# A chunked recurrence beside a convolution: the order of VectorE's work inside a round

## The reference, cut to what matters

```
# convolution branch
z = za * sigmoid(zb)
z = conv over time(z, conv_w[31 taps]) + conv_b        # each channel by itself

# recurrence, for each head, S is 64 x 64
for t in range(512):
    Sa = S @ a_t                                        # a = -kk
    S  = S * w_t + outer(Sa, b_t) + outer(v_t, k_t)     # b = kk * a
    y_t = S @ r_t
y = group_norm(y) * gn_g + gn_b
out = ((y + (sum(r * k * r_k)) * v) * g) @ w_o
```

## Time and profile before

| | us |
|---|---|
| median of 3 runs | 3665.07 (3653.8 to 3669.39) |
| the profiled execution, its own time | 3657.74 |
| its span in the trace | 3655.9 |
| the stage of the recurrence with its warm-up, from the trace's times | some 680 (2340 to 3020) |
| busy over the whole span: PE / DVE / ACT / POOL | 3305.3 / 2015.0 / 1299.8 / 374.7 |

### The profile page before, as it was taken

One profiled execution on the slowest core, in us unless ns is written; L12 is line 12 of the kernel. 1 busy time (PEld: TensorE's weight loads), 2 busy tenths in 40 slices (PEclk: granted clock), 3 DMA queues, 4 the chain that ended last, 5 costly groups with the idle time before them and its releaser, 6 DMA issues.

```text
span 3655.9 us, 51894 instructions
## 1 busy us (share of the span) xinstructions
PE 3305.3 (90%) x21498; PEld 2605.7 (71%) x21498; DVE 2015.0 (55%) x3571; ACT 1299.8 (36%) x2143; POOL 374.7 (10%) x334
## 2 busy tenths in 40 slices
PE   6898899999899999998986889879999889989998
PEld 4667777777585677777765666567777777768886
DVE  5455356653432466654555437678778762554443
ACT  3234232222223342223333135456555533323221
POOL 0001000000000000000001000055445420000000
PEclk9899899999898999999997989989999989999999
DMA  3220023442551124432310220221111102233231
GB/s 126 61 69 2 24 93 128 132 133 68 85 99 42 37 96 138 138 115 69 127 46 26 62 87 12 75 61 39 45 41 40 45 5 87 81 110 104 93 99 62
DMA packets 318856, 274.78 MB, mean 75 GB/s; under 512 B 10912, under 2 KB 310048, under 8 KB 317856
## 3 DMA queue, kind: packets, MB, share of 16 engines
q1 hardware_dynamic: 314368, 256.07, 23.2%
q10 hardware_dynamic: 4256, 15.40, 1.1%
HBM read 265.16 MB, written 6.29 MB: 74 GB/s over the span
## 4 chain that ended last, share of the span: by engine, by line
PE 76%; DVE 13%; ACT 6%; issue 3%; POOL 1%; DMA 1%; DVEq 0%; ACTq 0%; SPq 0%; POOLq 0%
PE ps L95 74%; DVE f L107 4%; DVE f L101 3%; DVE r L101 3%; ACT f L88 2%; PE ps L98 2%; ACT f L92 1%; ACT r L92 1%; DVE f L104 1%; ACT f L89 1%; ACT L88 1%; POOL f L101 1%; DVE f L113 1%; DVE f L110 1%; DMA f<-in_w_in_odd 0%
## 5 line engine op out<-in xcount | busy, mean ns | idle before, releaser
L95 PE MATMUL ps<-r,r 128*128 128x512 f32 x10368 | 2459.2, 396 | 124.8 <-DVE r L101 87.3
L95 PEld LDWEIGHTS ps<-r,r 128*128 128x128 f32 x10368 | 1925.1, 190 | 601.7 <-issue 182.9
L95 PE MATMUL ps<-f,f 64*64 64x64 f32 (+9 forms) x10192 | 809.2, 270 | 181.2 <-ACT f L92 45.9
L101 DVE TENSOR_TENSOR r<-f,r 128x1024 fp32r<-128x1024 f32 (+2 forms) x621 | 657.4, 1064 | 461.7 <-ACT r L92 454.1
L95 PEld LDWEIGHTS ps<-f,f 64*64 64x64 f32 (+3 forms) x10192 | 601.7, 157 | 363.0 <-issue 168.8
L92 ACT ACTIVATE r<-f 128x1024 fp32r<-128x1024 f32 (+2 forms) x548 | 506.6, 937 | 783.4 <-PE ps L95 661.1
L101 POOL TENSOR_TENSOR f<-f,f 128x256 f32<-128x256 f32 (+1 forms) x276 | 331.3, 1213 | 478.5 <-ACT f L88 267.7
L107 DVE SCALAR_TENSOR_TENSOR f<-f,f,f 128x128 f32<-128x128 f32 (+3 forms) x622 | 365.7, 593 | 26.5 <-ACT f L88 7.3
L101 DVE TENSOR_TENSOR f<-ps,f 128x512 f32<-128x512 f32 (+7 forms) x333 | 180.4, 554 | 339.5 <-PE ps L95 329.9
L92 ACT ACTIVATE f<-ps 128x256 f32<-128x256 f32 (+3 forms) x422 | 183.7, 451 | 512.9 <-PE ps L95 364.9
L88 ACT ACTIVATE f<-ps 128x512 f32<-128x512 f32 (+3 forms) x203 | 112.0, 553 | 621.5 <-PE ps L95 619.4
(11 more groups left out here) (33 smaller groups left out, 733.3 us busy)
## 6 DMA issues: line engine op xcount, KB each, us to landing
f<-in_w_mlp_up SPq DMA_DIRECT2D x32, 1024.0 KB, 6.0
f<-in_w_mlp_down SPq DMA_DIRECT2D x32, 1024.0 KB, 6.1
f<-in_w_ff SPq DMA_DIRECT2D x32, 1024.0 KB, 5.2
f<-in_w_ada SPq DMA_DIRECT2D x48, 512.0 KB, 3.9
f<-in_w_in SPq DMA_DIRECT2D x24, 1024.0 KB, 5.0
f<-in_w_in SPq DMA_DIRECT2D x44, 512.0 KB, 3.6
f<-in_w_in_even SPq DMA_DIRECT2D x12, 1024.0 KB, 5.2
f<-in_w_in_odd SPq DMA_DIRECT2D x12, 1024.0 KB, 12.8
```

Of the source, the lines that this page charges most:

```text
L95: return self.e.matmul(out, l, r, start=first, stop=last)
L101: return self.e.tensor_tensor(out, a, b, op)
```

## The change

One line: the tuple that orders VectorE's kinds of phase within a round. No instruction is added or taken away on any engine, and the queues of TensorE, ScalarE, GpSimd and SyncE are the same.

```
-    DVE = ("c", "out", "xy", "tm", "fin", "tap", "ct", "p", "g", "i0", "cf", "proj")
+    DVE = ("xy", "c", "tm", "fin", "ct", "p", "i0", "cf", "proj", "out", "g", "tap")
```

## The result

| | before | after |
|---|---|---|
| median (lowest to highest) | 3660.81 us (3650.59 to 3673.52, 16 runs) | 3674.94 us (3667.63 to 3686.65, 16 runs) |
| the profiled execution, its own time | 3657.74 | 3672.75 |
| its span | 3655.9 | 3671.0 |

The change makes the kernel 14.1 us slower, a ratio of 1.0040 (95% interval 1.0029 to 1.0052). The direction was forecast, the size was not: 3691 was predicted, +26 us on the median shown then. The effect lies within the 0.5% that the prediction took as the bound of what can be told apart; sixteen runs of each still separate it from nothing.

What follows compares the result with a forecast made beforehand. TensorE was taken to set the pace, VectorE's chain in rounds of kind 6 to 10, both in turn from round 84. Terms 12 + 6 + 2 + 6 = +26 us gave a median of 3691, range 3655 to 3712.

Steps and rivals of the forecast that it cites:

- PSUM bank: Rounds 41, 29, 53, 65, 77: transposes wait 1.2 us for `out`, now behind the low half, to free their bank; +6 us.
- vectors behind a tap (kinds 0 to 2): Round 37 and its like: the previous round's tap delays the state's vectors, costing TensorE 0.4 us each, +2 us.
- sets' gaps: TensorE's waits before `y` and `tm` of round 47 and its like: `tm` 2.0 us later in each, +12 us.
- updates from 84: Rounds from 84, without filler: 11 updates of 0.67 us now stand ahead of the state's vectors, +7.4 us.
- `out` from 84: Rounds 88, 94, 100 and 106: `out` no longer stands ahead of the updates, -1.7 us.
- The chain without meetings: VectorE's work in rounds 42 to 46, before changes in GpSimd's blocking: `y` moves by +1.27 us, `tm` by +0.2.
- The meetings: GpSimd's adds blocking VectorE in rounds 42 to 46, up to 1.47 us each; `tm` between -1.4 and +3.1, +2.0 taken.
- Six sets: Stretches of twelve rounds, each with one gap like that before round 47; 2.0 us lost in each, +12 us.
- The last rounds: Rounds from 84, where no filler is left and TensorE and VectorE take turns: +6 us, bounds 0 and +12.
- The much slower one: Rival: both GpSimd blockings in every set, vectors stop TensorE twice, other terms at upper bounds; +44 us, 3709, chance 0.15.
- "Faster": Rival: urgent work comes first, so the gap before round 47 shrinks by 2.5 us, -15 in six; 3650, chance 0.15.
- "Nothing": Rival: taps move into VectorE's idle time and TensorE's gap absorbs lateness of rounds 44 and 45; +5, 3670, chance 0.20.

Runs made afterwards that it cites:

- `out` alone: The kernel before with only `out` moved to the end of VectorE's round: 3666.52 us against 3659.8, ratio 1.0017.
- The two kernels without adds: The kernels before and after, each with GpSimd's convolution adds cut to 8 of 512 columns: 3603.48 us and 3610.91 us, one run each.
- The single moves: The kernel before with only `out` moved last, only the updates ahead of the vectors, or only the tap last: ratios 1.0017, 1.0018 and 1.0015.
- one experiment: The kernel after with the state's vectors put back ahead of the updates: 3669.78 us against 3654.68 for the kernel before, ratio 1.0038.

## Why the prediction was right in direction and too large

Against the sum, step by step:

| term | forecast | measured | |
|---|---|---|---|
| PSUM bank | +6 | +5.9 | right, place and size |
| vectors behind a tap (kinds 0 to 2) | +2 | +1.3 | right in kind |
| sets' gaps | +12 | +7.1 | mis-sized; this is the step that failed |
| updates from 84 | +7.4 | +6.0 | right in place, a little large |
| `out` from 84 | -1.7 | -1.75 | right in sum, in two places and not four |
| other rounds from 84 | 0 | -3.1 | not in the sum |
| end of the stage | +26 | +15.6 | |

- *The bank.* The rows of round 40 and 41 and the count of banks gave 1.2 us; five steps of 1.15 to 1.19 came, with `out` alone as with the whole change, and went when `out` was put ahead of the low half.
- *The chain without meetings.* +0.2 per set for `tm` was computed. The two kernels without adds differ by 0.2 on average, but from -0.3 to +1.2 by set, and the terms of the sum (waits of 0.42, one tap more) cost rounds 43 to 45 nothing there, so the agreement is luck.
- *The meetings.* The step that failed is "I take +2.0", nearer the upper bound "since two of the meetings can be named". Both named meetings are in the trace (1.79 for the tap of round 42, 2.56 for `pE`). What was not counted are the meetings that ended: VectorE is busy for 6 us less in rounds 24 to 83. In the set shown a product of round 44 and the low half were held up before, and are less or not at all now. Before:

```profile
2670.98 1.11 DVE L107 SCALAR_TENSOR_TENSOR f<-f,f,f 128x256 f32<-128x256 f32 x1
2674.35 1.67 DVE L101 TENSOR_TENSOR r<-f,r 128x1024 fp32r<-128x1024 f32 x1
```

  After:

```profile
2678.02 0.77 DVE L107 SCALAR_TENSOR_TENSOR f<-f,f,f 128x256 f32<-128x256 f32 x1
2680.80 1.21 DVE L101 TENSOR_TENSOR r<-f,r 128x1024 fp32r<-128x1024 f32 x1
```

  I looked at the taps and `pE` alone, and not at what else GpSimd had held up. In place of 2.0 per set 1.43 remained, between 0.88 and 1.84: 1.6 in rounds 43 to 45, less what the rounds behind gave back. The row of 87 that I called taps also holds other instructions of that shape; by the program 64 of them are taps.
- *Six sets.* I multiplied by six; the sum over the sets before round 24 is +0.05. Five have the gap in full flow. That is 2 of the 4.9 us; the size per set is the other 2.9.
- *The last rounds.* Rounds 86, 90, 92, 96, 98, 102 and 104 are longer, by 6.0 us together, which is the updates. `out` gave back 0.87 and 0.88 in rounds 94 and 106, and nothing in 88 and 100, where four times 0.42 was set. What the sum lacked is the clock: 1.45 us in round 95, and 0.9 in rounds 109 to 111, whose window has 0.62 before and 0.95 after. The sum took every wait at its own length, while here the same matmuls ran at another clock. The term's lower bound of 0 held, for a reason that I had not given.
- *The rivals.* The much slower one needed every set at the upper bound of 3.1, and none came above 1.84. "Faster" rested on the gap shrinking: it did shrink (34.2 to 31.6 us), and the loss stood in front of it, in waits for the vectors. "Nothing" said that the gap takes up what is late in rounds 44 and 45; in part it does, as the kernel with the tap last shows (gap 4.61 for 5.77), and the argument with which I set it aside was too strong. Measured +14 lies midway between its +5 and the forecast.
- *The base.* The three runs shown had a median of 3665.07; sixteen give 3660.81. 4.3 of the 16 us between 3691 and 3674.94 is that.

The bank's 5.9 is shown by putting `out` in and out of its place in both kernels. That the sets' loss starts in rounds 43 to 45 and comes with the tap's place is shown by four kernels with the tap last, which all have it, and four other orders, which don't. That it takes GpSimd's adds is shown by the pair without them, from one run each; the way they act is argued. The single moves leave 3.8 us unexplained. That it is the updates' place together with the others is supported by one experiment, and why the gap gives back less then is open.

## What to carry to other kernels

On an in-order engine that is a bottleneck in only some rounds, one order for all rounds is the wrong tool: list what stands between the previous result that TensorE took and the next one that it waits for, in the rounds with the gap alone, and take out whatever nobody waits for. Here that was a group norm, a tap and `out`, worth 10 to 15 us, while the reordering of every round cost 14. When work is moved behind a slow instruction, look for the small instruction that frees a buffer: a 0.42 us `out` behind a 1.2 us cast cost 5.9 us. And a model of who meets whom has to count the meetings that end as well as those that begin.

## What the runs showed of the hardware

- GpSimd's 128x512 adds of fp32 hold up VectorE more widely than I had assumed. `TENSOR_SCALAR` on 128x4, with one SBUF input, takes 0.166 us without the adds and 1.005 with them; the scan 0.69 and 1.10; `RECIPROCAL` on 128x4 takes 0.178 in both. The prediction cited only the case of two SBUF inputs; the Trainium skill ("SBUF — State Buffer", section "SBUF: two separate sides") also names VectorE operations in a mode that uses both ports, and the 128x4 row agrees with that. No run shows in which mode the instruction ran.
- Cutting these adds made the kernel 3654.68 - 3603.48 = 51 us faster by one run, more than any order of VectorE's work gave. No run here tried to do the adds elsewhere.
- TensorE's granted clock in one round was worth 1.45 us between two kernels with the same wait of 1.80 us ahead of it. In a total it can pass for the effect of an edit; round by round the two can be told apart.
